# One stage for memory keys, values and queries: norms applied to the products in PSUM, three fp32r products for keys and values

## What is computed

```
def rmsnorm(x, g):
    y = xf * lax.rsqrt(jnp.mean(xf * xf, axis=-1, keepdims=True) + NORM_EPS)
    return (y * g.astype(F32)).astype(x.dtype)

def memory_kv(mem, mem_norm_g, w_mk, w_mv):      # mem (1, 256, 2048), weights (2048, 512)
    m = rmsnorm(mem, mem_norm_g)
    return ((m @ w_mk).reshape(B, M, MEM_HEADS, MEM_HEAD_DIM),
            (m @ w_mv).reshape(B, M, MEM_HEADS, MEM_HEAD_DIM))

def memory_attend(h, mem_k, mem_v, w_mq, w_mo):  # h = rmsnorm(x, ln_mem_g)
    q = (h @ w_mq).reshape(B, S, MEM_HEADS, MEM_HEAD_DIM)
    ...
```

## Time and profile before

| | us |
|---|---|
| median of 3 runs | 2326.09 |
| lowest and highest | 2318.37, 2332.95 |
| the profiled execution, its own time | 2328.1 |
| its span in the profile | 2326.5 |

### The profile page before, as it was taken

The page is one execution under the profiler, slowest core; times in us unless marked ns, Lnnn a source line. Parts: engine busy times, 40 slices in busy tenths (PEclk is TensorE's granted clock), DMA queues, the critical chain, the costliest instruction groups (busy, mean ns, idle before and its releaser), DMA issues. The chain is left out here.

```text
span 2326.5 us, 38595 instructions
## 1 busy us (share of the span) xinstructions
PE 1984.1 (85%) x15938; PEld 1341.8 (58%) x15938; DVE 687.9 (30%) x1304; ACT 541.6 (23%) x870; POOL 143.4 (6%) x180
## 2 busy tenths in 40 slices
PE   6999977896878876979379699999999999999994
PEld 6999966664465545974365355444445555444452
DVE  4357756223333333340433311111111111111112
ACT  4446522221112222220221211111101111111112
POOL 0000003000122210000000000000000000000000
PEclk9999986797779998999699799999999999999997
DMA  7544510112132316630534699999999999999994
GB/s 218 148 127 127 136 24 12 39 34 91 38 105 77 106 45 197 172 139 21 154 109 199 235 408 416 409 419 411 418 410 419 411 417 416 415 412 415 421 411 162
DMA packets 217888, 543.42 MB, mean 234 GB/s; under 512 B 44376, under 2 KB 167866, under 8 KB 182576
## 3 DMA queue, kind: packets, MB, share of 16 engines
q1 hardware_dynamic: 209410, 532.97, 60.7%
q0 software_dynamic: 7936, 8.68, 1.7%
q10 hardware_dynamic: 438, 0.32, 0.1%
HBM read 524.86 MB, written 28.59 MB: 238 GB/s over the span
## 5 line engine op out<-in xcount | busy, mean ns | idle before, releaser
L2570 PE MATMUL p_g<-w_expert,xgT 128*64 128x256 f32 x2048 | 246.8, 396 | 41.8 <-DVE xgT L2626 41.8
L2587 PE MATMUL p_y<-w_expert,hidT 128*64 128x512 f32 x1024 | 226.8, 595 | 24.0 <-DVE hidT L2636 24.0
L2570 PE MATMUL p_u<-w_expert,xgT 128*64 128x256 f32 x2048 | 232.2, 379 | 0.0
L2570 PEld LDWEIGHTS p_g<-w_expert,xgT 128*64 128x64 f32 x2048 | 155.4, 143 | 116.0 <-issue 54.8
L2570 PEld LDWEIGHTS p_u<-w_expert,xgT 128*64 128x64 f32 x2048 | 151.9, 137 | 69.1
L2541 PE MATMUL p_xg<-low,slot_sel 128*64 128x512 f32 x792 | 177.4, 597 | 4.0 <-DVE slot_sel L2600 4.0
L2587 PEld LDWEIGHTS p_y<-w_expert,hidT 128*64 128x64 f32 x1024 | 70.6, 137 | 159.6 <-issue 128.0
L2541 PEld LDWEIGHTS p_xg<-low,slot_sel 128*64 128x64 f32 x792 | 58.9, 138 | 102.5 <-issue 94.0
L2654 ACT ACTIVATE act_g<-p_g 128x256 f32<-128x256 f32 x32 | 12.3, 383 | 434.0 <-PE p_u L2570 434.0
L2673 POOL DMA_INDIRECT x_dram<-y_slots,row x32 | 49.9, 1558 | 1011.9 <-DVE y_slots L2638 1011.9
L605 PE MATMUL in_acc<-x_high,w_in_high 128*128 128x320 f32 (+2 forms) x560 | 93.8, 320 | 8.2 <-ACT w_in_high L637 8.2
(11 more groups left out here) (567 smaller groups left out, 2782.5 us busy)
## 6 DMA issues: line engine op xcount, KB each, us to landing
w_expert<-in_w_gate_dram SPq DMA_DIRECT2D x64, 2048.0 KB, 12.0
w_expert<-in_w_up_dram SPq DMA_DIRECT2D x64, 2048.0 KB, 13.5
w_expert<-in_w_down_dram SPq DMA_DIRECT2D x64, 2048.0 KB, 12.2
w_in_raw<-in_w_in_dram SPq DMA_DIRECT2D x32, 1024.0 KB, 5.8
lat<-in_cache_kv_latent_dram SPq DMA_DIRECT2D x128, 128.0 KB, 2.1
w_out_raw<-in_w_out_dram SPq DMA_DIRECT2D x16, 1024.0 KB, 7.1
w_mk<-in_w_mk_dram SPq DMA_DIRECT2D x1, 4096.0 KB, 14.5
w_mv<-in_w_mv_dram SPq DMA_DIRECT2D x1, 4096.0 KB, 24.9
```

The costliest lines, as they stand in the source:

```text
L2570: mm = pe.matmul(acc[SL * h:SL * h + SL, 0:FF // 2], xgT[:, t, g // 2, :], w[g][:, FF * t + FF // 2 * h:FF * t + FF // 2 * h + FF // 2], s ...
L2587: mm = pe.matmul(p_y[SL * h:SL * h + SL, 512 * b:512 * b + 512], hidT[:, k % 2, k // 2, :], w[4 + k // 2][:, D * (k % 2) + 1024 * h + 512 ...
```

## The change

`memory_keys` and `memory_queries` are gone, with both calls of `feature_norm` around them. In their place stands one block, `memory_in`, with 12 parts of weights of 1 MB each: parts 0 to 3 are a quarter (4 of 16 feature tiles) of `w_mk` with all 512 columns, 4 to 7 the same of `w_mv`, 8 to 11 are 128 columns of `w_mq`. Every part is cast to fp32r by ACT (`whi`, two buffers) and its rest is made by DVE (`wlo`, two buffers); there are four raw buffers. The memory tokens and `xT` are multiplied by their gains only, and split the same way. Their norms are computed beside that and applied when the products leave PSUM: one number per partition for keys and values (`keep`), one per column for the queries (`keep_queries`). The sum over partitions for the memory tokens is gone (ACT's accumulator does it, tokens being on the partitions); that for `xT` is one matmul of the summed squares.

The diff, cut to its core. In the parts left out, a cast or rest of part c (`split(c)`) waits for its load, and from c = 2 on for `used` to reach c - 1; the four router loads of SP stand behind the stores of keys and values; and the old block of SP alone is gone, its `mem_k_s` loads being issued in `memory_prompt`:

```diff
-def memory_queries(nc, d, S):
...
-def memory_keys(nc, d, S, outs):
...
+def memory_weights(d, c):
+    if c < 8:
+        return d[('w_mk', 'w_mv')[c // 4]][0].rearrange("(t p) n -> p t n", p=128)[:, 4 * (c % 4):4 * (c % 4) + 4, :]
+    return d['w_mq'][0].rearrange("(t p) n -> p t n", p=128)[:, :, 128 * (c - 8):128 * (c - 8) + 128]
...
+def memory_in(nc, d, S, outs):
+    PARTS = 12
...
+                for c in range(2, PARTS):
+                    if c >= 4:
+                        sp.wait_ge(w_low, c - 3)
+                    sp.dma_start(weight_view(raw[c % 4], c), memory_weights(d, c)).then_inc(S.mem_w_in[c % 4], 16)
...
+                        sp.wait_ge(kv_kept, 2 * x + i + 1)
                         sp.dma_start(outs[4 + x][0, 0, 128 * i:128 * i + 128].rearrange("p h n -> p (h n)"), buf[:, i, :]).then_inc(out, 16)
+                sp.dma_start(S.w_router[:, :, 0:NG], d['w_router_c'][0].rearrange("(t p) n -> p t n", p=128)).then_inc(S.router_in, 16)
...
+                pe.wait_ge(S.mem_in, 16)
+                for k in range(8):
+                    if k >= 4:
+                        pe.wait_ge(mem_low, 2 * (k - 4) + 2)
+                    for t in range(2):
+                        for i in range(2):
+                            ins = pe.transpose(p_t[k % 4][:, 256 * t + 128 * i:256 * t + 128 * i + 128], S.mem_tokens[:, i, 128 * (2 * k + t):128 * (2 * k + t) + 128], S.ident)
+                    ins.then_inc(turned, 1)
...
+                    def products(m, w, first, last):
+                        for i in range(2):
+                            for t in range(4):
+                                ins = pe.matmul(p_kv[2 * x + i][:, :], m[:, 4 * q + t, 128 * i:128 * i + 128], w[:, t, :], start=(first and t == 0), stop=(last and t == 3))
+                        return ins
+                    pe.wait_ge(w_high, c + 1)
+                    pe.wait_ge(mem_high, 4 * q + 4)
+                    products(mem_hi, hi, q == 0, False)
+                    pe.wait_ge(mem_low, 4 * q + 4)
+                    products(mem_lo, hi, False, False)
+                    pe.wait_ge(w_low, c + 1)
+                    products(mem_hi, lo, False, q == 3).then_inc(used, 1)
+                    if c == 6:
+                        pe.wait_ge(kv_kept, 2)
+                        for h in range(MEMH):
+                            for i in range(2):
+                                ins = pe.transpose(p_kt[h // 2][:, 256 * (h % 2) + 128 * i:256 * (h % 2) + 128 * i + 128], mem_k[:, i, 128 * h:128 * h + 128], S.ident)
+                            if h % 2:
+                                ins.then_inc(k_turned, 1)
+                pe.wait_ge(x_added, 8)
+                pe.matmul(p_sum[:, 0:T], S.table("ones"), total[:, 0:T], start=True, stop=True).then_inc(x_summed, 1)
+                pe.wait_ge(x_high, DT)
+                for k in range(MEMH):
...
+                def tokens_high(k):
+                    act.wait_ge(turned, k + 1)
+                    for t in range(2):
+                        act.activation(mem_hi[:, 2 * k + t, :], p_t[k % 4][:, 256 * t:256 * t + 256], ACT.Copy, scale=g_mem[:, 2 * k + t:2 * k + t + 1]).then_inc(mem_high, 1)
...
+                def x_squares(q):
+                    for n in (2 * q, 2 * q + 1):
+                        if n > 1:
+                            act.wait_ge(x_added, n - 1)
+                        if n == 0:
+                            act.wait_ge(mem_squared, 4)
+                        act.activation((total, part)[min(n, 1)], S.xT[:, 2 * n:2 * n + 2, :].rearrange("p t n -> p (t n)"), ACT.Square).then_inc(x_squared, 1)
+                def x_high_part(q):
+                    for t in range(4 * q, 4 * q + 4):
+                        act.activation(x_hi[:, t, :], S.xT[:, t, :], ACT.Copy, scale=g_x[:, t:t + 1]).then_inc(x_high, 1)
+                split(0)
+                for k in range(4):
+                    tokens_high(k)
+                split(1)
+                for k in range(4, 8):
+                    tokens_high(k)
+                token_squares()
+                for c in range(2, PARTS):
+                    split(c)
+                    if c == 2:
+                        token_root()
+                    if 2 <= c < 6:
+                        x_squares(c - 2)
+                        x_high_part(c - 2)
+                    if c == 9:
+                        act.wait_ge(x_summed, 1)
...
+                def add(n):
+                    dve.wait_ge(x_squared, n + 1)
+                    dve.tensor_tensor(total, total, part, ALU.add).then_inc(x_added, 1)
+                    dve.wait_ge(x_added, n)
+                def keep(x, buf):
+                    dve.wait_ge(used, 4 * x + 4)
+                    dve.wait_ge(mem_inverted, 1)
                     for i in range(2):
+                for k in range(3):
+                    tokens_low(k)
+                split(0)
+                for k in range(3, 8):
+                    tokens_low(k)
+                split(1)
+                dve.wait_ge(mem_squared, 4)
+                dve.tensor_reduce(mem_sum[:, :], mem_ss[:, :, :], AX.X, ALU.add).then_inc(mem_summed, 1)
+                for c in range(2, PARTS):
+                    split(c)
+                    if 2 <= c < 6:
+                        for n in (2 * (c - 2), 2 * (c - 2) + 1):
+                            if n:
+                                add(n)
+                        x_low_part(c - 2)
+                    if c == 2:
+                        dve.wait_ge(mem_rooted, 1)
+                        dve.reciprocal(mem_inv[:, :], mem_root[:, :]).then_inc(mem_inverted, 1)
+                    if c == 5:
+                        keep(0, mem_k)
+                    if c == 6:
+                        dve.tensor_tensor(total[:, 0:T], total[:, 0:T], total[:, T:2 * T], ALU.add).then_inc(x_added, 1)
+                    if c == 9:
+                        for n in range(2):
+                            dve.wait_ge(k_turned, n + 1)
+                            dve.tensor_copy(S.mem_kT[:, 2 * n:2 * n + 2, :].rearrange("p h n -> p (h n)"), p_kt[n][:, :]).then_inc(kT_kept, 1)
+                        keep(1, S.mem_v)
+                        dve.wait_ge(x_rooted, 1)
+                        dve.reciprocal(x_inv, x_root).then_inc(x_inverted, 1)
+                    if c >= 10:
+                        keep_queries(c - 10)
+                keep_queries(2)
+                keep_queries(3)
...
+                for b in range(NB):
+                    sp.dma_start(S.mem_k_s[:, b, :, :], d['cache_mem_k'][0, b].rearrange("(i p) h n -> p i (h n)", p=128)).then_inc(S.msk_in, 16)
...
+            S.mem_tokens = low[:, 0:2 * D].rearrange("p (i n) -> p i n", i=2); S.mem_in = sem("mem_in"); S.mem_w_in = [sem(f"mem_w_in{i}") for i in range(4)]
...
+                    sp.dma_start(S.mem_tokens, d['mem_prompt'][0].rearrange("(i p) n -> p i n", p=128)).then_inc(S.mem_in, 16)
+                    for c in range(2):
+                        sp.dma_start(weight_view(S.spare_late[c], c), memory_weights(d, c)).then_inc(S.mem_w_in[c], 16)
+            project_out(nc, d, S)
+            S.recycle(nc)
+            memory_in(nc, d, S, outs)
...
-                feature_norm(nc, S, "norm_mem", S.xT[:, :, :], mix[:, :, :], S.vec("ln_mem"), DT, D)
-                memory_queries(nc, d, S)
```

More of the change, by code:

```diff
@@ L795, in project_out @@
                 lambda sp: sp.dma_start(S.xT[:, :, :].rearrange("p t n -> p (t n)"), S.xT_dram).then_inc(x_in, 16))
-def memory_queries(nc, d, S):
-    w = d['w_mq'][0].rearrange("(t p) n -> p t n", p=128)
-    with ExitStack() as ctx:
-        raw = S.spare_late + [ctx.enter_context(nc.sbuf_tensor(f"w_mq_raw{i}", [128, DT, 128], F32)) for i in range(2)]
-        project(nc, S, "w_mq", S.mix, lambda c, m: w[:, :, c:c + m], 0, [(128 * k, 128) for k in range(MEMH)], raw,
-                lambda eng, copy, k, bank: copy(S.mem_q[:, k, :], bank[:, 0:T]), True)
 FULL = HP * T
@@ L1999, in memory_keys @@
-        mem_k = sb("mem_k", [128, 2, 512])
-        bank = [ctx.enter_context(nc.psum_tensor(f"pm_kv{i}", [128, 512], F32)) for i in range(4)]; p_kt = [ctx.enter_context(nc.psum_tensor(f"pm_kt{i}", [128, 512], F32)) for i in range(2)]
-        made = sem("mkv_made"); copied = sem("mkv_copied"); k_turned = sem("mk_turned"); k_kept = sem("mk_kept"); out = sem("mkv_out")
+        sem = lambda n: S.semaphore(nc, "mi_" + n)
+        spare = S.mix[:, :, :].rearrange("p t n -> p (t n)")
+        raw = S.spare_late + [spare[:, 0:D], sb("mi_raw", [128, D])[:, :]]
@@ new lines, in memory_in @@
+        whi = [sb(f"mi_high{i}", [128, D], FR) for i in range(2)]; wlo = [sb(f"mi_low{i}", [128, D], FR) for i in range(2)]
+        mem_hi, mem_lo = sb("mi_mem_high", [128, DT, MEM], FR), sb("mi_mem_low", [128, DT, MEM], FR)
+        x_hi, x_lo = sb("mi_x_high", [128, DT, T], FR), sb("mi_x_low", [128, DT, T], FR)
+        squares = spare[:, D:D + 4 * T]; total, part = squares[:, 0:2 * T], squares[:, 2 * T:4 * T]
```

(11 more changed lines are left out.)

135 lines of the change are left out of this document (61 added, 74 removed).

## The result

The changed kernel takes 2258.21 us (median of 4 runs, 2253.72 to 2259.2), the kernel before took 2323.74 in the same comparison (4 runs, 2318.37 to 2332.95). The ratio is 0.9702, with a 95% interval of 0.9677 to 0.9726: 3% faster. The forecast of 2263.3 is 5.1 us too slow, and its range holds the time. The profiled execution took 2259.2, with a span of 2257.6.

A forecast was written before the change was run, and what follows sets the result against it. Barrier-separated stages that don't overlap were taken as the bound, 158.96 us in this stretch. Head 9.9, clock 2.1, products 44.3, waits 4.0 and tail made 90.8; saving 68.2, less 5.4 for loads, gave 2263.3 us, range 2253 to 2277.

The forecast's parts named there:

- head, to part 0: Start of the new block, from PE's first transpose of the memory tokens to part 0's first product: 9.9 us.
- slow clock at its start: Part 0 starts after ten thin microseconds, so not at full clock: 2.1 us charged.
- products, 8 parts: Keys and values: eight parts of 24 fp32r products of 512 columns, 0.231 us each, 44.3 us.
- waits for ACT, parts 5 and 6: PE waits for ACT's late casts, 1.8 and another 2.1 us, 4.0 in all; its only expected waits.
- keys turned, sum, queries, rest: Block's tail: key transposes 0.9, sum 0.5, queries 28.3, last scaling 0.5, handover 0.3 us.
- stage: From PE's first transpose of the memory tokens to the first product of `memory_prompt`: 90.8 us, against 158.96.
- 2.1 MB ahead, at `project_out`: Two weight parts loaded ahead of `project_out`'s weights on the same queue delay its start: 5.4 us, 4.8 to 7.0.
- sum against before: Whole kernel: 68.2 us saved, 5.4 paid for the loads ahead, so the median falls by 62.8.
- sign of 88 to 96: Sign of a right forecast: first transpose to first product of `memory_prompt` takes 88 to 96 us.
- ACT and DVE didn't take over: Rival in the new block: slower highs, lows and squares give ACT a period of 8.1 us; total 2271, chance 0.15.
- PE did not stay at the lower clock: Rival: PE, waiting in each part, stays at lower clock through the block; products and queries double, total 2330, chance 0.03.
- The products kept their rate at 512 columns: Rival: 512-column fp32r products run like whole fp32 ones, 0.86 us, adding 117; total 2380, chance 0.02.

The follow-up runs named there:

- e_sp_block_b: Changed kernel with the old block of SP alone (`mem_k_s` loads, then router loads) put back before `memory_prompt`; 2278.65 us, 0.981 of the kernel before.
- e_no_ahead: Changed kernel with weight parts 0 and 1 loaded at the start of `memory_in`, not ahead of the output projection; 2261.15 us, 0.9719 of the kernel before.
- e_two_parts: Changed kernel with two buffers for the squares of x in place of one; 2252.27 us, 0.9693 of the kernel before.
- e_head: Changed kernel with DVE making the tokens' group 3 low parts before part 0's subtraction; 2259.22 us, 0.971 of the kernel before.
- e_loads_late: Changed kernel with memory tokens and parts 0 and 1 loaded behind the projection's last weight tile, SP's block before it gone; 2244.77 us, 0.9664 of the kernel before.
- e_two_products_b: Changed kernel without the product of the tokens' low part with the high weights for keys and values; 2252.82 us, 0.9706 of the kernel before.

## Why the prediction was right

The mechanism was as forecast: ACT's period sets two waits, at the parts named, and everything else of the block lies under PE. The number owes something to chance, as the clock shows below. By its steps, forecast and measured in us:

| step | forecast | measured |
|---|---|---|
| head, to part 0 | 9.9 | 8.5 |
| slow clock at its start | 2.1 | 0 |
| products, 8 parts | 44.3 | 44.4 |
| waits for ACT, parts 5 and 6 | 1.8 + 2.1 | 1.60 + 1.70 |
| keys turned, sum, queries, rest | 30.5 | 30.5 |
| stage | 90.8 | 86.76 |
| 2.1 MB ahead, at `project_out` | +5.4 | +6.25 |
| sum against before | -62.8 | -65.7 |

**The head** was laid out too late by 1.4: the transposes of the last group began at 1031.45, 8.1 us after the first, and part 0 at 8.5. The subtraction was in the way, as said, but its neighbours were shorter: the last transposes took 0.41 where I had 0.9 at the lower clock, eight high parts of the tokens took 3.02 us, 0.38 each, where I had 0.43, and six low parts 2.44, 0.41 each for 0.48.

**The clock.** This term failed outright in this run: all windows read 1.00. e_sp_block_b, with the same code and the same idle times in its head, lost 1.6 us there. Of the eleven traces of the new block, part 0 starts at full pace in nine (2.07 to 2.09 us for its first 8 products, or the like of it where the product is another) and slowly in two, e_sp_block_b (2.90) and e_no_ahead (3.34). So the charge is right in kind, and comes or doesn't come. With it the stage would have been 88.4 to 88.9, inside the sign of 88 to 96; without it 86.76 is outside.

**The products** measured 0.227, between the two ends of 0.215 and 0.235, and below the 0.231 taken. 192 of them are 43.5; the products behind waits bring the stretch to 44.4. *TensorE: Matmul & The Clock Gate* (Trainium skill, Back-to-back issue gap) gives 0.216 for 512 columns, for a matmul by itself; for a stream of weight loads and matmuls, which is what runs here, the same section gives 0.131. The trace agrees with neither: it is 0.011 above the first, and by the same 0.011 at 320 columns (0.147 against 0.136). What stands above columns over 2.4 GHz is therefore 13 ns at both widths, and doesn't grow with them. That is where my scaling by columns went wrong.

**The waits** came at the two parts named, for the engine named, within 0.4 each; ACT's period was 7.45, forecast 7.6. The leads ahead of them fit too: the cast of part 3 ended 2.2 us early (forecast 2.4), that of part 4 0.2 (0.3). e_two_parts shows the cause by removing it. One term was missing from ACT's list, the four squares of the memory tokens, 1.06 us each and 4.7 in all. It did no harm by luck: the plan had the cast of part 2 wait for part 0, and the squares ended at 1037.57, just as part 0 did (its last row starts at 1035.61 and takes 1.98). e_head shows that they were as much of a bound: part 0 came 2.2 earlier, and the cast of part 2 only 0.3.

*ScalarE: Activation LUTs* (Trainium skill, What ACT_TABLE_LOAD costs) adds a drain to the load; here cast, load and root follow each other in 0.02 us (1039.59 to 1039.61, 1040.89 to 1040.90), so this load shows 1.28 and no drain.

**The loads ahead** cost 6.25, inside the 4.8 to 7.0, for 5.4 forecast. The queue's part of it, 5.18, is even less than 5.4 (2.1 MB in 5.18 us are 405 GB/s, against the 387 taken from another stage). What was put at nothing is the 1.07 us by which the longer block of SP holds the others. The forecast also missed that this cost was not the change's alone: the 2.1 MB of `mem_tokens`, which both kernels issue there, and the block around them cost another 5.1 (e_loads_late), already paid in the earlier trace rows.

**The rivals.** ACT and DVE didn't take over, but one product less would have let them (e_two_products_b). PE did not stay at the lower clock: it read 1.00 in this trace. The products kept their rate at 512 columns, far below the 0.58 us from which the change would have lost. The experiment with fp32 products shows how little hung on the rate: even at 0.859 us for a whole fp32 matmul, the new layout keeps 65 of 72 us.

**The other signs.** PE had no idle time before the queries, and no load released anything inside the block. The first product of `project_out` was to come near 913 and came at 906.28; with the code ahead no quicker than in the trace of before it would have been 913.9.

Where the 72.2 us of the stage come from, as far as runs show: 7.4 the kind of product, 16.4 SP's block. The other 48 are norms, splits and copies that now lie under products, and the passes that are gone, among them some 17 us of PE's sums over the partitions by the traces; no run parts these from each other.

## What to carry to other kernels

When stages follow one another through barriers and each is bound by another engine, look for work of one to lay under the other, and for passes that can go, before looking for faster instructions: here the kind of product was a tenth of the gain. Issue loads for a later stage behind the last loads of the running one, not ahead of its first: the 4.2 MB ahead of the projection and the block that issued them cost 11.3 us of PE's time, and the same loads issued some 40 us ahead of their use cost 0.4 at most, which is within the spread of that stretch (116.7 to 118.0). And lay out the period of the engine that feeds PE: a single buffer between ACT and DVE was all that stood behind the last 4 us.

## What the runs showed of the hardware that was not expected

- The time of a DMA issue depends on what the queue holds: `w_router_f`, 128-byte rows, took 8.13 and 9.37 us behind 4 MB of `mem_k_s`, 1.18 and 1.21 with nothing large before it.
- The same idle times of PE (2.43, 1.64, 2.33 in the head) passed at a granted clock of 1.00 in one execution and gave 0.72 in 1036 to 1042 in another (2.90 us for 8 products instead of 2.09).
- A fp32r matmul of 512 columns costs 0.227 us, one of 320 columns 0.147: both about 13 ns above columns over 2.4 GHz. Three of them (0.68) take four fifths of one fp32 matmul (0.859).
